# Chunk decays of a bidirectional state-space scan: the backward exponent copied over the forward one, one exponential a head

## The reference, cut to what matters

```
def segsum_exp(a):
    cs = jnp.cumsum(a, axis=-1)
    diff = cs[..., :, None] - cs[..., None, :]
    return jnp.exp(jnp.where(mask, diff, -jnp.inf))      # mask: lower triangle
...
    Lmat = segsum_exp(a)
    y_diag = jnp.einsum('bclgn,bcsgn,bgrcls,bcsgrp->bclgrp', Cc, Bc, Lmat, xd)
...
    y_f = ssd_scan(xs, dt_f, A[0], Bm, Cm)
    y_b = flip(ssd_scan(flip(xs), flip(dt_b), A[1], flip(Bm), flip(Cm)))
    y = y_f + y_b + xs * d_skip.astype(jnp.float32)[:, None]
```

## Time and profile before

| | |
|---|---|
| median of 3 runs | 2930.65 us |
| profiled execution, first to last instruction | 2927.1 us |
| TensorE busy in it | 2844.0 us (97%) |
| VectorE / ScalarE / GpSimd busy | 1921.0 / 1161.9 / 442.2 us |
| mean granted TensorE clock | 0.984 of full |
| diag stage, first exponent to last `y` evacuated | 454.6 to 531.6 us |
| TensorE idle in that stage, waits of 1 us or more | one, 1.0 us |

### The profile page before, as it was taken

The page is one execution under the profiler, slowest core; times in us unless marked ns, Lnnn a source line. Parts: engine busy times, 40 slices in busy tenths (PEclk is TensorE's granted clock), DMA queues, the critical chain, the costliest instruction groups (busy, mean ns, idle before and its releaser), DMA issues.

```text
span 2927.1 us, 34428 instructions
## 1 busy us (share of the span) xinstructions
PE 2844.0 (97%) x13489; PEld 2265.7 (77%) x13489; DVE 1921.0 (66%) x2492; ACT 1161.9 (40%) x1708; POOL 442.2 (15%) x323
## 2 busy tenths in 40 slices
PE   8999999999999999999999999999799999999999
PEld 6767778767778888877767888888676888887887
DVE  6548866656587666765667766776737866666254
ACT  2223325213343333433245565556624433334342
POOL 0420011360004332202000000000000232222020
PEclk7999999999999999999999999999999999999999
DMA  6344475025132222375540111111133222226453
GB/s 216 110 136 151 145 224 194 29 79 201 54 131 80 75 86 87 124 251 183 176 157 18 47 43 43 43 43 45 64 101 101 87 86 87 87 65 203 136 158 116
DMA packets 361686, 326.60 MB, mean 112 GB/s; under 512 B 11501, under 2 KB 319182, under 8 KB 361486
## 3 DMA queue, kind: packets, MB, share of 16 engines
q1 hardware_dynamic: 348486, 271.61, 29.7%
q0 software_dynamic: 12000, 48.61, 4.5%
q10 hardware_dynamic: 1040, 4.19, 0.4%
HBM read 263.88 MB, written 68.35 MB: 114 GB/s over the span
## 4 chain that ended last, share of the span: by engine, by line
PE 90%; DVE 5%; ACT 2%; DMA 1%; issue 1%; POOL 1%; SPq 0%; ACTq 0%; DVEq 0%; POOLq 0%
PE psum_gemm L1953 20%; PE psum_misc L1953 18%; PE psum_gemm L2399 8%; PE psum_gemm L216 6%; PE psum_gemm L217 6%; PE psum_gemm L220 6%; PE psum_misc L2463 3%; PE psum_gemm L2484 3%; PE psum_gemm L2472 3%; PE psum_gemm L318 2%; PE psum_misc L216 2%; PE psum_misc L217 2%; PE psum_misc L220 2%; PE psum_misc L888 1%; PE psum_gemm L2485 1%
## 5 line engine op out<-in xcount | busy, mean ns | idle before, releaser
L216 PE MATMUL psum_gemm<-h_hi,w_hi 128*128 128x512 f32 x816 | 329.3, 404 | 12.0 <-DVE h_lo L401 8.2
L217 PE MATMUL psum_gemm<-h_lo,w_hi 128*128 128x512 f32 x816 | 318.5, 390 | 0.0
L198 ACT ACTIVATE w_hi<-w_raw 128x1024 fp32r<-128x1024 f32 x93 | 97.8, 1055 | 455.1 <-PE psum_gemm L220 321.4
L1878 DVE TENSOR_TENSOR ring_lo<-piece_raw,ring_hi 128x512 fp32r<-128x512 f32 x192 | 137.0, 722 | 206.2 <-ACT ring_hi L1872 205.7
L220 PE MATMUL psum_gemm<-h_hi,w_lo 128*128 128x512 f32 x816 | 251.9, 390 | 0.0
L203 DVE TENSOR_TENSOR w_lo<-w_raw,w_hi 128x1024 fp32r<-128x1024 f32 x93 | 119.1, 1285 | 158.5 <-ACT w_hi L198 158.5
L1872 ACT ACTIVATE ring_hi<-piece_raw 128x512 fp32r<-128x512 f32 x192 | 112.7, 593 | 246.2 <-PE psum_misc L1953 208.3
L1953 PE MATMUL psum_misc<-h_hi,ring_hi 128*128 128x512 f32 x512 | 200.6, 392 | 0.6 <-DVE ring_lo L1878 0.6
L216 PEld LDWEIGHTS psum_gemm<-h_hi,w_hi 128*128 128x128 f32 x816 | 153.2, 188 | 61.5 <-issue 20.8
L1953 PE MATMUL psum_misc<-h_hi,ring_lo 128*128 128x512 f32 x512 | 199.4, 389 | 0.0
L1953 PE MATMUL psum_misc<-h_lo,ring_hi 128*128 128x512 f32 x512 | 199.2, 389 | 0.0
(11 more groups left out here) (422 smaller groups left out, 6792.3 us busy)
## 6 DMA issues: line engine op xcount, KB each, us to landing
ada_w<-in_w_ada SPq DMA_DIRECT2D x28, 1024.0 KB, 5.5
w_raw<-in_f_w_up SPq DMA_DIRECT2D x52, 512.0 KB, 4.9
ffn_act_scratch<-gate_act SPq DMA_DIRECT2D x42, 512.0 KB, 2.6
piece_raw<-in_f_w_down SPq DMA_DIRECT2D x80, 256.0 KB, 3.2
piece_raw<-ffn_act_scratch SPq DMA_DIRECT2D x80, 256.0 KB, 2.9
pair_raw<-in_f_w_up SPq DMA_DIRECT2D x36, 512.0 KB, 5.1
w_raw<-in_e_w_in SPq DMA_DIRECT2D x29, 512.0 KB, 4.5
x_scratch<-x_res SPq DMA_DIRECT2D x3, 4096.0 KB, 12.6
```

The source lines that it names most:

```text
L198: act.activation(w_hi[:, s], w_raw[:, s], ACT.Copy).then_inc(s_hi, 1)
L216: pe.matmul(o, wh, rh[:, k, c], start=(k == 0), stop=False)
L217: pe.matmul(o, wh, rl[:, k, c], start=False, stop=False)
L1878: dve.tensor_tensor(Al[:, idx % 7, 0:n], src, Ah[:, idx % 7, 0:n].bitcast(F32), ALU.subtract).then_inc(s_wl, 1)
```

## The change

The two directions share one exponential. The backward exponent is written over the forward one with a predicated copy on VectorE (`copy_predicated`), under a mask `above` that is one where the partition's position is later than the target, from `backward` in `pG[:, 0]` into `forward(h)`. `forward(h)` is `pG[:, 1]`, from head 7 on for odd heads `pM[:, 0]`. The mask products (L1459 before) go, and with them the constants `mask_r` and `ident_r`. ScalarE then takes one exponential of `forward(h)`, and there is no sum of directions. The waits change with it: the forward exponent of head h waits for the exponential of head h - 1 (heads 1 to 6), of head h - 2 (from 8), or for the second evacuation (head 7); the backward one waits for the predicated copy of head h - 1. The exponential waits for the copy of its own head. The weights of head h - 1 are multiplied after the copy of head h. The `y` of a head from 2 on has only two half buffers in turn, in `pM[:, 1]`, so it waits for the evacuation two heads before instead of four.

The diagonal holds only the forward term after the copy. The backward one is dt (backward) times the score on the diagonal, and it goes into the skip weight: GpSimd multiplies the scores by the identity (two 128 x 1024, into `y_S` as scratch), VectorE sums them (`own_dve`, in head 2), multiplies by dt and adds `d_skip` (tile `own_weight`), and GpSimd multiplies x by that weight for each head (16 of 128 x 512, into `y_S`) where VectorE did it in the evacuation. The evacuation is now `y_S` plus the product. The constants on GpSimd become three fewer instructions.

The 18 new instructions stand ahead of `x_w`, in the middle of the heads. The core of the diff:

```diff
@@ -1180,13 +1179,13 @@
...
-        mask = at("mask", AR + 65, [P, 2, P])
-        maskR = at("mask_r", AR + 66, [P, 2, P], F32R)
-        identR = at("ident_r", AR + 67, [P, P], F32R)
+        above = at("above_diagonal", AR + 66, [P, P])
+        y_w = at("own_weight", AR + 72, [P, CH, 16])
+        g_own = at("own_score", AR + 72.5, [P, SSM_GROUPS, CH])
...
@@ -1206,7 +1205,7 @@
...
-        E_ = at("decays", 32, [P, 2, 2, SEQ])
+        E_ = at("decays", 32, [P, 2, SEQ])
...
@@ -1419,46 +1416,58 @@
...
-        def diff(d):
-            return pG[:, 1 - d]
+        def forward(h):
+            return pM[:, 0] if h >= 7 and h % 2 else pG[:, 1]
+
+        backward = pG[:, 0]
+
+        def y_ps(h):
+            return pM[:, int(h >= 2), (h % 2) * HALF:(h % 2) * HALF + HALF]
 
         def diag_pe(pe):
             def y_of(h):
                 if h >= 4:
-                    pe.wait_ge(s_yev, h - 3)
+                    pe.wait_ge(s_yev, h - 1)
...
                 pe.wait_ge(s_M, h + 1)
-                ps = pM[:, (h % 4) // 2, (h % 2) * HALF:(h % 2) * HALF + HALF]
+                ps = y_ps(h)
...
+
+            def exponent(h, d):
+                hd = 16 * d + h
+                dst = backward if d else forward(h)
+                for n in range(2):
+                    pe.matmul(dst[:, n * HALF:(n + 1) * HALF], selR[:, hd:hd + 1].to_broadcast([P, P]),
+                              T2[:, n * HALF:(n + 1) * HALF], start=True, stop=False)
+                for n in range(2):
+                    pick = pickR[:].rearrange("p (c h) -> p c h", h=8)[:, 4 * n:4 * n + 4, h % 8:h % 8 + 1]
+                    last = pe.matmul(dst[:, n * HALF:(n + 1) * HALF], csbT[:, 2 * d + h // 8],
+                                     pick.to_broadcast([P, 4, P]), start=False, stop=True)
+                last.then_inc(s_dif[d], 1)
...
             for h in range(SSM_HEADS):
-                for d in range(2):
-                    hd = 16 * d + h
-                    if h >= 1:
-                        pe.wait_ge(s_exp, 2 * h - 1 + d)
-                    elif d:
-                        ev_in_wait(pe, U_OUTB + 1)
-                    for n in range(2):
-                        pe.matmul(diff(d)[:, n * HALF:(n + 1) * HALF], selR[:, hd:hd + 1].to_broadcast([P, P]),
-                                  T2[:, n * HALF:(n + 1) * HALF], start=True, stop=False)
-                    for n in range(2):
-                        pick = pickR[:].rearrange("p (c h) -> p c h", h=8)[:, 4 * n:4 * n + 4, h % 8:h % 8 + 1]
-                        pe.matmul(diff(d)[:, n * HALF:(n + 1) * HALF], csbT[:, 2 * d + h // 8],
-                                  pick.to_broadcast([P, 4, P]), start=False, stop=False)
-                    for n in range(2):
-                        last = pe.matmul(diff(d)[:, n * HALF:(n + 1) * HALF], identR[:],
-                                         maskR[:, d:d + 1].to_broadcast([P, 4, P]), start=False, stop=True)
-                    last.then_inc(s_dif[d], 1)
+                if h == 7:
+                    pe.wait_ge(s_yev, 2)
+                elif h > 7:
+                    pe.wait_ge(s_exp, h - 1)
+                elif h:
+                    pe.wait_ge(s_exp, h)
+                exponent(h, 0)
+                if h:
+                    pe.wait_ge(s_sum, h)
+                else:
+                    ev_in_wait(pe, U_OUTB + 1)
+                exponent(h, 1)
                 if h == 0:
                     scores_pe(pe, 1)
...
@@ -1476,11 +1485,10 @@
...
             for h in range(SSM_HEADS):
-                for d in range(2):
-                    if h >= 2:
-                        act.wait_ge((s_sum, s_M)[d], h - 1)
-                    act.wait_ge(s_dif[d], h + 1)
-                    act.activation(E_[:, h % 2, d], diff(d), ACT.Exp).then_inc(s_exp, 1)
+                if h >= 2:
+                    act.wait_ge(s_M, h - 1)
+                act.wait_ge(s_sum, h + 1)
+                act.activation(E_[:, h % 2], forward(h), ACT.Exp).then_inc(s_exp, 1)
                 if h < 2:
                     scores_act(act, h)
 
@@ -1490,32 +1498,69 @@
...
+            pool.wait_ge(s_sp, 17)
+            for g in range(SSM_GROUPS):
+                pool.wait_ge(s_gm, g + 1)
+                pool.tensor_tensor(yS[:, g].rearrange("p (c q) -> p c q", c=CH), Gm[:, g].rearrange("p (c q) -> p c q", c=CH),
+                                   ident[:].rearrange("p (o q) -> p o q", o=1).to_broadcast([P, CH, P]), ALU.mult
+                                   ).then_inc(s_own, 1)
+            pool.wait_ge(s_ownw, 5)
+            pool.wait_ge(s_ex, 3)
+            for x in range(2):
+                pool.wait_ge(s_zs[x], 64)
+            for h in range(SSM_HEADS):
+                q = slice(h * 64, (h + 1) * 64)
+                pool.tensor_tensor(yS[:, :, q], xS[:, :, q], y_w[:, :, h:h + 1].to_broadcast([P, CH, 64]), ALU.mult
+                                   ).then_inc(s_own, 1)
+
+        def own_dve(dve):
+            dve.wait_ge(s_lndt, 5)
+            for g in range(SSM_GROUPS):
+                dve.wait_ge(s_own, g + 1)
+                dve.tensor_reduce(g_own[:, g], yS[:, g].rearrange("p (c q) -> p c q", c=CH), mybir.AxisListType.X, ALU.add
+                                  ).then_inc(s_ownw, 1)
+            for g in range(SSM_GROUPS):
+                h = slice(HPG * g, HPG * (g + 1))
+                dve.wait_ge(s_ownw, g + 1)
+                dve.tensor_tensor(y_w[:, :, h], dtS[:, :, 16 + HPG * g:16 + HPG * (g + 1)],
+                                  g_own[:, g].rearrange("p (c o) -> p c o", o=1).to_broadcast([P, CH, HPG]), ALU.mult
+                                  ).then_inc(s_ownw, 1)
+            dve.wait_ge(s_ownw, 4)
+            dve.tensor_tensor(y_w[:], y_w[:], dskip[:].rearrange("p (o h) -> p o h", o=1).to_broadcast([P, CH, 16]), ALU.add
+                              ).then_inc(s_ownw, 1)
 
         def diag_dve(dve):
 
             def evac(h):
                 dve.wait_ge(s_y, h + 1)
-                ps = pM[:, (h % 4) // 2, (h % 2) * HALF:(h % 2) * HALF + HALF].rearrange("p (c q) -> p c q", c=CH)
-                dve.scalar_tensor_tensor(yS[:, :, h * 64:(h + 1) * 64], xS[:, :, h * 64:(h + 1) * 64],
-                                         dskip[:, h:h + 1], ps, ALU.mult, ALU.add).then_inc(s_yev, 1)
+                dve.wait_ge(s_own, SSM_GROUPS + h + 1)
+                o = yS[:, :, h * 64:(h + 1) * 64]
+                dve.tensor_tensor(o, o, y_ps(h).rearrange("p (c q) -> p c q", c=CH), ALU.add).then_inc(s_yev, 1)
+
+            def weights(h):
+                dve.wait_ge(s_exp, h + 1)
+                if h % HPG == 0:
+                    dve.wait_ge(s_gm, h // HPG + 1)
+                if h >= 4:
+                    dve.wait_ge(s_y, h - 3)
+                dve.tensor_tensor(W_[:, h % 4], E_[:, h % 2], Gm[:, h // HPG], ALU.mult).then_inc(s_M, 1)
             for h in range(SSM_HEADS):
                 if h in (1, 2):
                     b_copy(dve, h - 1)
                 if h == 3:
                     mods_dve(dve)
-                    dve.wait_ge(s_ex, 3)
-                    for x in range(2):
-                        dve.wait_ge(s_zs[x], 64)
-                dve.wait_ge(s_exp, 2 * h + 2)
-                dve.tensor_tensor(E_[:, h % 2, 1], E_[:, h % 2, 1], E_[:, h % 2, 0], ALU.add).then_inc(s_sum, 1)
+                for d in range(2):
+                    dve.wait_ge(s_dif[d], h + 1)
+                dve.copy_predicated(forward(h).rearrange("p (c q) -> p c q", c=CH),
+                                    above[:].bitcast(mybir.dt.uint32).rearrange("p (o q) -> p o q", o=1).to_broadcast([P, CH, P]),
+                                    backward.rearrange("p (c q) -> p c q", c=CH)).then_inc(s_sum, 1)
+                if h:
+                    weights(h - 1)
+                if h == 2:
+                    own_dve(dve)
                 if h >= 4:
                     evac(h - 4)
-                dve.wait_ge(s_sum, h + 1)
-                if h < 2:
-                    dve.wait_ge(s_gm, h + 1)
-                if h >= 4:
-                    dve.wait_ge(s_y, h - 3)
-                dve.tensor_tensor(W_[:, h % 4], E_[:, h % 2, 1], Gm[:, h // HPG], ALU.mult).then_inc(s_M, 1)
+            weights(SSM_HEADS - 1)
             for h in range(SSM_HEADS - 4, SSM_HEADS):
                 evac(h)
 
```

More of the change, by code:

```diff
@@ L35 @@
 LAM_INIT = 0.8 - 0.6 * float(np.exp(-0.3))
-MASKED = -float(2 ** 100)
 STRIP = 2048 - P
@@ L1235, in build @@
         s_eva = sem("output_evacuated")
+        s_own, s_ownw = sem("own_products"), sem("own_weights")
         s_gm = sem("scores_then_t_hi")
-        NC_CONST = 15
+        NC_CONST = 12
         def z_tile(j):
@@ L1253, in ssd_consts @@
             pool.memset(tri[:], 1.0).then_inc(s_sc, 1)
-            pool.memset(mask[:], 0.0).then_inc(s_sc, 1)
+            pool.memset(above[:], 0.0).then_inc(s_sc, 1)
             pool.memset(sel[:], 0.0).then_inc(s_sc, 1)
@@ L1259, in ssd_consts @@
```

(19 more changed lines are left out.)

## The result

The changed kernel took 2945.17 us (median of 4 runs, 2942.76 to 2946.67); the kernel before, run beside it, 2931.34 (4 runs, 2929.97 to 2933.78). The ratio is 1.0043 [1.0031, 1.0056]: slower by 13.8 us. I had forecast no change that a measurement could tell, 2934.4, in a range up to 2945.0. As timed, the kernel lies 0.2 us above that range. The ratio, applied to the 2930.65 that the forecast started from, gives 2943.3, just inside it. By either count the likeliest case was wrong: the difference is clear of noise, and about 10 us larger than the 3.8 that I had added up.

A forecast was written before the change was run, and what follows sets the result against it. TensorE was taken to bound the stage, with a head's latency now counting too. 9.25 (head 7 later) - 8.4 (later heads) + 0.9 (GpSimd) + 2.0 (end) = +3.8 us, so 2934.4 us; range 2928.5 to 2945.

The forecast's parts named there:

- the likeliest case: Whole kernel: no change that a measurement could tell, +3.8 us, 2934.4 us, alone 2932 to 2937; chance 0.41.
- The predicated copy: VectorE, each head: takes 1.23 us, the price of a PSUM copy of that size, without waiting for GpSimd.
- the first rival: The predicated copy takes two passes, 2.0 to 2.3 us: 13 to 17 us slower, 2944 to 2948; chance 0.22.
- Heads 7 to 15: With two forward buffers TensorE needs 3.59 us a head; nine heads give back 8.4 us.
- The term of 0.9: Later heads: weights' products waiting for GpSimd, mostly for x_w, delay y by 0.9 us in all.
- Head 7's start: First exponent of head 7 at 494.18 against 484.93 before: 9.25 us behind, from early waits and low clock.
- the modulation, 1.15 us: VectorE, before head 3's copy: the modulation keeps its old duration of 1.15 us.
- the wait that I had before head 5: Heads 0 to 6: a chain of 4.49 us a head leaves TensorE idle for 0.89 us.
- The two new gaps: Heads 1 and 2: TensorE idle 3.86 us each, each followed by about 3.4 us at half rate, 1.7 us lost.
- the second rival: Clock low for longer or also at head 4, or evacuations delayed by GpSimd: another 3 to 5 us, 2938 to 2940; chance 0.14.
- The end: Last y, behind head 15's exponents: waits for evacuations of 1.75 and 0.2 us, 2.0 us.
- Rivals three and four: Waits overlap, TensorE bound in all heads: -12.9 us, 2918, chance 0.05; clock and lock cost nothing: -0.5, 2930, chance 0.15.

The follow-up runs named there:

- The first: Changed kernel with VectorE's own-weight steps moved from head 2 to head 3, behind the modulation: 2934.99 us, ratio 1.0021 to the kernel before.
- the sixth experiment: Changed kernel without the backward diagonal term: no products on GpSimd, no own-weight steps on VectorE, plain skip weight in the evacuation; one execution, 2933.46 us.
- The other buffers: Changed kernel with the y of heads 13 and 14 written into the free forward buffer: 2937.24 us, ratio 1.0024 to the kernel before.
- the two kernels built on the new orders: Changed kernel with copies of B, modulation and own weights later, late y in free buffers, 2928.16 us; and that with the second forward buffer from head 5, 2926.77 us.

## Why the prediction was right or wrong, step by step

**The predicated copy: right.** Its 11 rows with the destination in `pG` and the 5 with it in `pM` agree:
```profile
L1554 DVE COPY_PREDICATED psum_gemm<-above_diagonal,psum_gemm 128x1024 f32<-128x1024 uint32 x11 | 13.5, 1226 | 10.8 <-PE psum_gemm L1450 10.8
...
L1554 DVE COPY_PREDICATED psum_misc<-above_diagonal,psum_gemm 128x1024 f32<-128x1024 uint32 x5 | 6.1, 1229 | 3.1 <-PE psum_gemm L1450 3.1
```
I took 1.23, the price of the nearest row, and the first rival, which needed more than 1.5 us, has fallen. It did not wait for GpSimd either: 1.21 and 1.23 at 483.22 and 489.49, in the middle of the products. That rival would have given the right total, 2944 to 2948, from a cause that isn't there. Its chance widened my range to where the time nearly lay; that is luck of the width and no understanding.

**Heads 7 to 15: right.** From 501.67 to 530.25 there are eight heads, 3.57 us each; 3.59 was forecast, and the nine heads gave back the 8.4 us. The weights' products took up to 1.97 beside GpSimd, where up to 2.5 was forecast, but all of that before head 7, where VectorE had slack: GpSimd was through with the 16 products at 495.3 and with `x_w` at 500.1, not at 509. The term of 0.9 was 0.

**Head 7's start: 9.25 forecast, 16.3 measured** (501.67 - 484.74, less the 0.6 by which the stage started later). The 484.93 of the prediction is from the chain of waits, whose rows begin where the row before them ends; in the timeline the same matmul starts at 484.74:
```profile
484.74 0.71 PE L1452 MATMUL psum_gemm<-cs_rows,sel_r 128*128 128x512 f32 x2
```
This is the term that failed, in two places. First, "the modulation, 1.15 us": I had written that two-input operations wait for GpSimd, had priced that for the weights' products alone, and had started the products at 477, just before the modulation, in the same paragraph. The two facts stood beside each other and I did not put them together. By the rule of the Trainium skill ("SBUF — State Buffer", Who interferes with whom: the one that issues first keeps the shared port pair for its whole instruction and the other is blocked) the cost of a wait is set by the partner's length, not by one's own. The trace agrees: 1.02 us, the distance of two products, for an operation that takes 0.16 alone. It was paid by five operations of the eleven, 4.0 us in all. Head 4 started 3.4 us later than forecast for it, at 485.61 where 482.2 would have answered to my 481.62. The first and the sixth experiment, which take the products away from there in two ways, both bring the gap down to 1.6. Second, the other 3.5 us between head 4 and head 7 are the clock: the window from 485.6 to 495.0 has TensorE busy at 0.52, 9.4 us of work for 4.9. Of these 4.5 us 0.9 took the place of the wait that I had before head 5.

**The clock: the mechanism was right, the size not.** "The two new gaps ... about 3.4 us at half rate" holds for those two: the stretches 467 to 471 and 474 to 478. That more falls would come, and longer ones, was in the second rival, at another 3 to 5 us; there were two more, which took 4.5 and about 5 us within the stage. I had taken the length of a fall from two places of the trace before as if it were a constant; in these kernels falls in the stage lasted 3.4 us, once 6.8, or 10.2 to 13.7. The trace before could have told me. A third place, behind a gap of 3.6 us at 1559.4, I had left out:
```profile
1559.40:1563.00 3.60, 0.00 (x0) 0.00 (x0) 3.31 (x4) 1.17 (x2) 0.00 (x0) 0.90 0.00 0
1563.00:1569.50 6.50, 6.15 (x25) 4.99 (x26) 4.39 (x10) 2.77 (x6) 0.00 (x0) 0.53 0.01 3
```
That fall is about twice as long as the ones that I counted with, and the same trace has one of 10.2 us from 2210.8 on. The filled kernels show that it is the clock: with the same chain and 43 matmuls more the stage is 9.6 us shorter.

**The end: 2.0 forecast, 6.3 measured.** The first wait was 1.38 against 1.75, and the second, 0.2, did not come; behind it, three `y` at half rate. I had given the gaps of 3.9 a fall and this one none, because my two rows had gaps of 2.5 and 3.9. The other buffers, which take the wait away, take the fall away too.

**The sum.** 16.3 - 8.4 + 0 + 6.3 = 14.2 in place of 9.25 - 8.4 + 0.9 + 2.0 = 3.8. By the other side: waits 15.5, where I had 15.3, minus 14.9 of matmuls, and lost clock of about 12.6 where I had 3.4 (busy time by one minus the clock, in the windows: 1.5, 1.7, 4.5, and 4.9 up to 545.45). The last 1.0 is, by my estimate, the ends of rows: a `y` in front of a wait lasts 1.89 where the next matmul follows after 1.70 if nothing waits, and there are six waits. The waits agree in total by cancellation: 5.60 came for 2.04, and 0.77 once for the three 0.9 behind it. So the total idle time was right by luck, and what was missing from the sum is what follows idle time. Rivals three and four, that the waits overlap or that clock and lock cost nothing, have fallen. The second, with 0.14, came nearest: it had a fall at head 4 and longer ones. Its other half, evacuations delayed by the products, did not happen (0.67 to 0.69 us each), the slow modulation stood in no rival, and its 3 to 5 us were less than half of the 10 that were missing.

**Open.** Of five profiles with a wait of 1.38 to 1.45 us before the third-last `y` three show a fall behind it (both of the changed kernel and the one with the late own weights) and two none (the one without own products and the one with the later copies of B). What decides, I can't say; the work before and behind it is nearly the same. Nor is it the length of the gap elsewhere: 1.57 us before head 2 brought no fall in four kernels and 1.57 before head 4 one of 3.4 us (without own products); 2.5 before head 3 brought none with the later copies of B and one of 10.2 in the two kernels built on the new orders. The fall at 2210.8 of the trace before has no gap in front of it at all: TensorE was busy for 4.98 of the 5 us up to 2211. Nor do the runs show what makes a fall last 3.4 or 13.7 us.

## What to carry to other kernels

Price an operation beside GpSimd by its inputs and the partner's duration, not by its own size: a row of short two-input operations on the critical chain is dear for its size, and what helped here was to let the partner start behind it. Price each new wait of TensorE with the low clock that can follow it, which here cost 12.6 us beside 15.5 of waits, and as a range, since the same wait cost different amounts in two executions; where a wait can't be avoided, matmuls that nobody reads can be cheaper than idling. And matmuls that go are only worth their time where the new chain of a head is shorter than the head's period; where it isn't, what the order of another engine puts in that chain (a copy of B, a modulation) decides more than what was removed.

## What the runs showed that I had not expected

- A CAST from SBUF to SBUF with one input (L1135, 8 columns) took part in the waiting too: 1.10 us for two beside GpSimd, 1.03 of it for one of them, and 0.24 for two without it.
- Not every short operation pays: of nine between 478.4 and 483.3 that read SBUF alone five waited for a product and four took about 0.16.
- Behind a gap of 1.38 or 1.39 us came falls of 10 to 14 us, in three of five profiles; the page's busy share of TensorE, 97% in both kernels, shows nothing of it.
- A reduction of 128x1024 to 8 columns takes 1.21 us, as much as a copy of that size.
